# Row norms scaled ahead of the transposes, three tiles deep

## The reference

```python
def rms_norm(x, g):
    xf = x.astype(jnp.float32)
    y = xf * lax.rsqrt(jnp.mean(xf * xf, axis=-1, keepdims=True) + NORM_EPS)
    return (y * g.astype(jnp.float32)).astype(x.dtype)
...
h = rms_norm(x, pre_norm_w[l])
p = h @ w_cat
...
hn = rms_norm_2(h, norm_g)
proj = hn @ w_in
```

## Time and profile before

| What | Value |
|---|---|
| Median of three runs | 3918.17 us |
| Profiled execution, own time | 3913.43 us |
| Its span, first to last instruction | 3911.4 us |
| PE busy | 3361.2 us (86%) |
| DVE busy | 1559.4 us (40%) |
| ACT busy | 1033.8 us (26%) |
| POOL busy | 382.6 us (10%) |
| Mean bandwidth of the transfers | 152 GB/s |

### The profile page before, as it was taken

One profiled execution on the slowest core, in us unless ns is written; L12 is line 12 of the kernel. 1 busy time (PEld: TensorE's weight loads), 2 busy tenths in 40 slices (PEclk: granted clock), 3 DMA queues, 4 the chain that ended last, 5 costly groups with the idle time before them and its releaser, 6 DMA issues. The chain is left out here.

```text
span 3911.4 us, 80384 instructions
## 1 busy us (share of the span) xinstructions
PE 3361.2 (86%) x33244; PEld 2811.4 (72%) x33244; DVE 1559.4 (40%) x2571; ACT 1033.8 (26%) x2007; POOL 382.6 (10%) x407
## 2 busy tenths in 40 slices
PE   7999999888869859999997699999967894988873
PEld 5877777788747749998996488888857873544441
DVE  3145653333336541114665255555433434111113
ACT  2122311122132120012454144455422110211112
POOL 0000000000000000000000122233111000222222
PEclk9999999999989979999998699999978996999997
DMA  3335455211244333233553211111004336999997
GB/s 108 97 115 200 156 199 185 87 52 45 95 167 130 133 94 92 87 97 121 174 171 122 98 33 39 40 50 39 25 21 155 127 101 242 417 419 418 412 415 301
DMA packets 315891, 594.55 MB, mean 152 GB/s; under 512 B 57281, under 2 KB 223018, under 8 KB 286646
## 3 DMA queue, kind: packets, MB, share of 16 engines
q1 hardware_dynamic: 267257, 465.55, 33.6%
q10 hardware_dynamic: 37476, 108.51, 7.9%
q0 software_dynamic: 10928, 17.08, 1.2%
HBM read 471.84 MB, written 139.97 MB: 156 GB/s over the span
## 5 line engine op out<-in xcount | busy, mean ns | idle before, releaser
L3145 PE MATMUL ex_bank_ps<-ex_w_gate_up_sb,ex_xT_sb 128*64 128x256 f32 x2240 | 292.3, 417 | 75.9 <-DMA ex_w_gate_up_sb<-in_w_up_e 68.2
L3145 PEld LDWEIGHTS ex_bank_ps<-ex_w_gate_up_sb,ex_xT_sb 128*64 128x64 f32 x2240 | 171.9, 145 | 208.3 <-issue 127.0
L260 DVE CAST in_w_hi_sb<-in_w_sb 128x1024 fp32r<-128x1024 f32 x119 | 82.0, 689 | 551.3 <-PE in2n_bank_ps L272 268.4
L1428 PE MATMUL mix_bank_ps<-mix_y_hi_sb,mix_wb_hi_sb 128*128 128x512 f32 (+2 forms) x480 | 171.5, 357 | 71.1 <-DVE mix_y_lo_sb L1619 56.0
L272 PE MATMUL in2n_bank_ps<-in_h_hi_sb,in_w_hi_sb 128*128 128x352 f32 (+3 forms) x696 | 224.9, 323 | 3.8 <-DVE in_h_lo_sb L384 3.8
L272 PE MATMUL in2n_bank_ps<-in_h_lo_sb,in_w_hi_sb 128*128 128x352 f32 (+3 forms) x696 | 224.3, 322 | 0.0
L272 PE MATMUL in2n_bank_ps<-in_h_hi_sb,in_w_lo_sb 128*128 128x352 f32 (+3 forms) x696 | 223.8, 322 | 0.0
L272 PE MATMUL qkv_tile_bank_ps<-in_h_hi_sb,in_w_hi_sb 128*128 128x352 f32 (+1 forms) x576 | 192.5, 334 | 8.1 <-DMA qkv_eps_sb<-const_rms_cols 7.5
L3336 DVE TENSOR_TENSOR ex_hidden_sb<-ex_silu_g_sb,ex_bank_ps 128x128 f32<-128x128 f32 x70 | 20.2, 288 | 442.6 <-ACT ex_silu_g_sb L3197 442.6
L272 PE MATMUL qkv_tile_bank_ps<-in_h_lo_sb,in_w_hi_sb 128*128 128x352 f32 (+1 forms) x576 | 185.5, 322 | 0.0
L272 PE MATMUL qkv_tile_bank_ps<-in_h_hi_sb,in_w_lo_sb 128*128 128x352 f32 (+1 forms) x576 | 185.3, 322 | 0.0
(11 more groups left out here) (467 smaller groups left out, 8213.1 us busy)
## 6 DMA issues: line engine op xcount, KB each, us to landing
ex_w_gate_up_sb<-in_w_gate_e SPq DMA_DIRECT2D x70, 1024.0 KB, 20.3
ex_w_gate_up_sb<-in_w_up_e SPq DMA_DIRECT2D x70, 1024.0 KB, 29.7
ex_w_down_sb<-in_w_down_e SPq DMA_DIRECT2D x70, 1024.0 KB, 29.4
in_w_sb<-in_w_in SPq DMA_DIRECT2D x118, 512.0 KB
scr_pT<-in_o_sb ACTq DMA_DIRECT2D x65, 512.0 KB
scr_p2T<-in_o_sb ACTq DMA_DIRECT2D x52, 520.0 KB
qkv_x_sb<-scr_p2T SPq DMA_DIRECT2D x8, 1560.0 KB
mix_gate_sb<-scr_pT SPq DMA_DIRECT2D x24, 512.0 KB, 3.4
```

What stands on the lines that cost most here:

```text
L260: dve.tensor_copy(self.w_hi[:, s, :, 0:width], w).then_inc(self.w_hi_rdy, 1)
L1428: last = pe.matmul(bank[:, 4 * s + c, 0:w], w_[:, s, k, :], y_[:, k0[n] + k, a:a + w], start=(k == 0 and z == 0), stop=(k == kts[n] - 1 an ...
L3145: last = t.matmul(bank[m * BT:(m + 1) * BT, GU_B + b % 2, 0:2 * P], xT[:, s, k, at:at + BT], wgu[:, ws, :, k, m::M], start=(k == 0), stop= ...
```

## The change

In both stages the tile is scaled by `rstd` and by the gain in one instruction of DVE, in token rows and ahead of the transposes. For this the gain is loaded as a row of 1024 numbers, broadcast to all partitions. ACT no longer scales. It casts the transposed tile from PSUM to `h_hi`. DVE subtracts `h_hi` from PSUM to give `h_lo`, so the intermediate `h` is gone.

The loads have four places, the scaled tiles three, the banks four pairs. ACT squares three tiles ahead of its casts, DVE scales three tiles ahead of its subtractions. SP issues the first tile ahead of the constants and leaves the second tile and the gain to ACT's queue. DVE splits the first weights after the first three scalings instead of after the last tile. The loops over tiles are written out.

The core of the diff follows. The call sites pass the gain as the plain vector, and the two arrays that held it in columns are gone.

```diff
     with ExitStack() as ctx:
         st = Stage(nc, ctx, name)
-        h = st.sb("h", [P, 2, KT, rows])
         ident = st.sb("ident", [P, P])
         rms_cols = st.sb("rms_cols", [P, 2])
-        gain_sb = st.sb("gain", [P, KT])
-        x_in = st.sb("x_in", [P, 2, D])
-        junk = st.sb("junk", [P, D])
-        ssq = st.sb("ssq", [P, 2])
-        ms = st.sb("ms", [P, 2])
-        rstd = st.sb("rstd", [P, 2])
-        xn = st.sb("xn", [P, 2, D])
+        gain_sb = st.sb("gain", [P, D])
+        XS, AHEAD = 4, 3
+        x_in = st.sb("x_in", [P, XS, D])
+        junk = st.sb("junk", [P, 2, D])
+        ssq = st.sb("ssq", [P, n_tiles])
+        ms = st.sb("ms", [P, n_tiles])
+        rstd = st.sb("rstd", [P, n_tiles])
+        xn = st.sb("xn", [P, AHEAD, D])
         bank = st.ps("bank", [P, 8, 512])
         consts = st.sem("consts_loaded")
-        x_ld = st.sems("x_loaded")
+        gain_ld = st.sem("gain_loaded")
+        x_ld = st.sems("x_loaded", XS)
         ssq_rdy = st.sem("ssq_ready")
         ms_rdy = st.sem("ms_ready")
         rstd_rdy = st.sem("rstd_ready")
         xn_rdy = st.sem("xn_ready")
         tr_done = st.sem("transposed")
         hT_rdy = st.sem("hT_ready")
-        h_step = st.sem("h_step")
+        hi_rdy = st.sem("h_high_ready")
         block = ctx.enter_context(nc.Block())
         for tiles, _, _ in stretches:
             tiles.psum = lambda s, n: bank[:, 4 * s + n, :]
@@ -331,88 +332,101 @@
                         step(tiles, i, u, width, after)
+        tokens = lambda t: slice(t * rows, (t + 1) * rows)
+
+        turned = lambda t, b: bank[:, 2 * (t % 4) + b, 0:4 * rows].rearrange("p (k r) -> p k r", k=4)
+        first, first_width, _ = stretches[0]
+
+        def load_x(eng, t):
+            if t >= XS:
+                eng.wait_ge(xn_rdy, t - XS + 1)
+            eng.dma_start(x_in[:rows, t % XS, :], src[tokens(t), :]).then_inc(x_ld[t % XS], 16)
+
         @block.sync
         def _(sp):
+            load_x(sp, 0)
+            sp.dma_start(rms_cols[:, :], rms_d).then_inc(consts, 16)
             sp.dma_start(ident[:, :], ident_d).then_inc(consts, 16)
...
+            load_x(sp, 2)
+            first.load(sp, 0, 0, first_width)
+            for t in range(3, n_tiles):
+                load_x(sp, t)
             each_tile(sp, lambda tiles, i, u, width, after: tiles.load(sp, i, u + 1, column=after))
         @block.scalar
         def _(act):
-            act.sem_inc(xn_rdy, 2)
+            load_x(act, 1)
+            act.dma_start(gain_sb[:, :], gain.rearrange("(a d) -> a d", a=1).broadcast_to([P, D])).then_inc(gain_ld, 16)
             stream.begin_store(act)
...
+
+            def square(t):
+                act.wait_ge(x_ld[t % XS], 16 * (t // XS) + 16)
+                act.activation(junk[:rows, t % 2, :], x_in[:rows, t % XS, :], ACT.Square, scale=D ** -0.5,
+                               accum_out=ssq[:rows, t:t + 1]).then_inc(ssq_rdy, 1)
+
+            for t in range(AHEAD):
+                if t >= 2:
+                    act.wait_ge(ssq_rdy, t - 1)
+                square(t)
+            for t in range(n_tiles):
+                act.wait_ge(tr_done, t + 1)
+                for b in range(2):
+                    last = act.activation(h_hi[:, 4 * b:4 * b + 4, tokens(t)], turned(t, b), ACT.Copy)
+                last.then_inc(hi_rdy, 1)
+                if t + AHEAD < n_tiles:
+                    act.wait_ge(ssq_rdy, t + AHEAD - 1)
+                    square(t + AHEAD)
             each_tile(act, lambda tiles, i, u, width, after: tiles.store(act, i, u, width))
             stretches[-1][0].end_store(act)
         @block.vector
         def _(dve):
-            dve.sem_inc(hT_rdy, 2)
             stream.begin_split(dve)
...
+
+            def scale(t):
+                dve.wait_ge(rstd_rdy, t + 1)
+                if t >= AHEAD:
+                    dve.wait_ge(tr_done, t - AHEAD + 1)
+                dve.scalar_tensor_tensor(xn[:rows, t % AHEAD, :], x_in[:rows, t % XS, :], rstd[:rows, t:t + 1], gain_sb[:rows, :],
+                                         ALU.mult, ALU.mult).then_inc(xn_rdy, 1)
+
+            dve.wait_ge(gain_ld, 16)
+            for t in range(AHEAD):
+                scale(t)
+            first.split(dve, 0, 0, first_width)
+            for t in range(n_tiles):
+                dve.wait_ge(hi_rdy, t + 1)
+                for b in range(2):
+                    last = dve.tensor_tensor(h_lo[:, 4 * b:4 * b + 4, tokens(t)], turned(t, b),
+                                             h_hi[:, 4 * b:4 * b + 4, tokens(t)].bitcast(F32), ALU.subtract)
+                last.then_inc(hT_rdy, 1)
+                if t + AHEAD < n_tiles:
+                    scale(t + AHEAD)
+
             each_tile(dve, lambda tiles, i, u, width, after: tiles.split(dve, i, u + 1))
         @block.gpsimd
         def _(pool):
...
+            pool.wait_ge(consts, 32)
+            for t in range(n_tiles):
+                pool.wait_ge(ssq_rdy, t + 1)
+                pool.tensor_tensor(ms[:rows, t:t + 1], ssq[:rows, t:t + 1], rms_cols[:rows, 0:1], ALU.add).then_inc(ms_rdy, 1)
+                pool.wait_ge(ms_rdy, t + 1)
+                pool.tensor_tensor(rstd[:rows, t:t + 1], ms[:rows, t:t + 1], rms_cols[:rows, 1:2], ALU.pow).then_inc(rstd_rdy, 1)
         @block.tensor
         def _(pe):
-            pe.sem_inc(tr_done, 2)
             stream.begin_product(pe)
...
+            pe.wait_ge(consts, 32)
+            for t in range(n_tiles):
+                pe.wait_ge(xn_rdy, t + 1)
+                if t >= 4:
+                    pe.wait_ge(hT_rdy, t - 3)
+                for k in range(KT):
+                    last = pe.transpose(turned(t, k // 4)[:, k % 4, :], xn[:rows, t % AHEAD, k * P:(k + 1) * P], ident[:rows, :rows])
+                last.then_inc(tr_done, 1)
+            pe.wait_ge(hT_rdy, n_tiles)
             each_tile(pe, lambda tiles, i, u, width, after: tiles.product(pe, i, u, width))
...
-        norm_project(nc, "in1n", x, SEQ, P, t["pre_norm_cols"], stream,
+        norm_project(nc, "in1n", x, SEQ, P, t["pre_norm_w"][0], stream,
...
-        norm_project(nc, "in2n", resid, LEN, ROWS, t["norm1_cols"], stream,
+        norm_project(nc, "in2n", resid, LEN, ROWS, t["norm1_g_2"][0], stream,
```

More of the change, by code:

```diff
@@ L350, in _ @@
         def _(act):
-            act.sem_inc(xn_rdy, 2)
+            load_x(act, 1)
+            act.dma_start(gain_sb[:, :], gain.rearrange("(a d) -> a d", a=1).broadcast_to([P, D])).then_inc(gain_ld, 16)
             stream.begin_store(act)
-            act.wait_ge(consts, 48)
-            with act.Fori(0, n_tiles // 2) as i:
-                for s in range(2):
-                    act.wait_ge(x_ld[s], i * 16 + 16)
-                    act.activation(junk[:rows, :], x_in[:rows, s, :], ACT.Square, scale=D ** -0.5,
-                                   accum_out=ssq[:rows, s:s + 1]).then_inc(ssq_rdy, 1)
-                    act.wait_ge(rstd_rdy, 2 * i + s + 1)
-                    act.wait_ge(tr_done, 2 * i + s + 1)
-                    act.activation(xn[:rows, s, :], x_in[:rows, s, :], ACT.Copy,
-                                   scale=rstd[:rows, s:s + 1]).then_inc(xn_rdy, 1)
+            def square(t):
[14 more added lines that the diff above has]
+                    square(t + AHEAD)
             each_tile(act, lambda tiles, i, u, width, after: tiles.store(act, i, u, width))
@@ L3433, in laid_out @@
     return {
-        "pre_norm_cols": columns(a["pre_norm_w"][0]),
         "conv_taps_cols": np.ascontiguousarray(a["conv_w"][0].T),
@@ L3439, in laid_out @@
         "rwkv_columns": np.ascontiguousarray(np.stack(per_channel + list(mu[:4 * C_BR].reshape(4, C_BR)), axis=1)),
-        "norm1_cols": columns(a["norm1_g_2"][0]),
         "conv2_taps_cols": np.ascontiguousarray(a["conv_w_2"][0].T),
```

41 lines of the change are left out of this document (removed).

## The result

The changed kernel takes 3897.31 us (median of five runs, 3888.25 to 3900.21). The kernel before took 3915.26 us in the five runs beside it (3910.63 to 3922.3). The medians differ by 17.95 us. The ratio is 0.995, with a 95% interval from 0.9937 to 0.9963, which is 19.6 us less, between 14.5 and 24.7. The forecast was 3892.6 us with a range from 3880 to 3905. The profiled execution took 3900.21 us with a span of 3898.4 us.

The account below looks back on a forecast made before the run. PE bounds the kernel, so each microsecond its first products start sooner is saved: 11.3 us in in1n and 14.3 in in2n make 25.6, from the median 3918.17 to 3892.6 us. The range was 3880 to 3905.

Parts of the forecast that it names:

- What bounds the stages: In in1n and in2n, latency rounds overlap with three tiles in flight, so DVE's work sets the pace; one round is 6.45 us.
- Pace: In the tile loops, DVE's scaling plus two subtractions take 2.65 us a tile in in1n and 2.45 in in2n.
- The start: At each stage's beginning, the first scaling waits for the gain, landing at 7.5 us in in1n (bounds 5.4 and 8.4).
- POOL beside DVE: In the first three tiles, DVE's scaling holds POOL's power and delays the next rstd: 1.1 us a stage.
- The first weights: In in1n, weights split before the first subtraction land at 9 to 10 us; DVE arrives at 12.4, so nothing waits.
- Sums: First products: in1n at 32.2 us, 11.3 sooner; in2n at 1451.2 us, 14.3 sooner.
- From the product to the kernel: Behind the first products, all waits only for PE, so the 25.6 us gained there shorten the whole kernel equally.
- Early clock: Rival: PE's clock rises during the denser transposes before the first products; 32 us saved, 3886 us; chance 0.20.
- Lock step by step: Rival: in both tile loops POOL always meets a DVE scaling; 14.0 us saved, 3904 us; chance 0.14.
- Time given back: Rival: a later stage waits on something that does not move, so time stays near 3915 us; chance 0.05.
- Slower weight stream: Rival: the experts' weights lie elsewhere in memory and stream slower; at 7% it costs 34 us, 3927 us; chance 0.04.

Follow-up runs that it names:

- e6: Changed kernel, but DVE instead of ACT casts the high part out of PSUM; 3913.51 us.
- e11: Changed kernel with squares, scalings and scaled tiles one ahead in place of three; 3964.56 us.
- e3: Changed kernel with squares, scalings and scaled tiles two ahead in place of three; 3898.95 us.
- e1: Changed kernel, but POOL waits only for its own small table and not for the identity matrix; 3887.37 us.
- e2: Changed kernel with all first loads on SP's queue, gain and second tile included; 3897.86 us.
- e5: Changed kernel with the gain copied once into PSUM by ACT and read there by the row scaling, transposes using three bank pairs; 3882.46 us.
- e4: Changed kernel with twelve unused transposes between the last tile's transposes and the first product; 3890.65 us.
- e9: Changed kernel with the edits of e1 and e5 and the twelve unused transposes of e4, in the gain's banks; median 3887.08 us, 0.9927 against the kernel before.
- e10: The changed kernel, unchanged, run again; median 3895.95 us of five runs, 0.9948 against the kernel before.

## Why the prediction was right

**What bounds the stages.** Right. DVE is full at three tiles ahead (9.60 of 9.60 us), more work on it costs its own length (e6), and fewer tiles ahead let the round show: 6.4 us for one tile (e11), 3.2 for each of two (e3), a tile of 2.39 us at three, where the round would allow 2.13.

**Pace.** 2.65 and 2.45 us were predicted, 2.39 and 2.19 measured. Each instruction has the length that the rows of before gave it: the scaling 1.28 us, the pair of subtractions 1.28 us. What failed is the adding of durations. In the timeline of `in1n` the scaling at 16.83 us takes 1.28 us, and the subtractions start at 18.02, 0.09 us before it ends; the next scaling starts at 19.22, 0.08 us before they end. The pair is 1.28 us and not 2 x 0.685. The term of 8 x 2.65 = 21.2 us was 2.1 us too large, and that of `in2n`, 10 x 2.45, 2.6 us.

**The start.** Mis-sized, and with the wrong event as the last one. I had the gain as the last to land, at 7.5 us. It landed 6.8 us after an issue at 1.18 us, within the bounds. But the first scaling started at 9.12 us: POOL's first sum waited for the identity matrix at 8.20 us, since both constants count on one semaphore. The mend (e1) puts the scaling at 7.96 us, on the gain. In `in2n` it is worse. There the first scaling comes 10.81 us after the stage's first issue, where 6.8 was predicted, and here are the two transfers that matter (KB, us from issue to landing):

```profile
in2n_gain_sb<-in_norm_g ACTq DMA_DIRECT2D x1, 512.0 KB, 8.9
...
in2n_ident_sb<-const_ident SPq DMA_DIRECT2D x1, 64.0 KB, 8.9
```

Both took 8.9 us, above my bound of 7.3 from the earlier trace rows. The prediction placed its 6.4 us between two rows by saying that the broadcast of 4.3 us ran nearly alone. It did not: over these 4.3 us the core's DMA engines were busy 0.91 of the time at 340 GB/s, and over the 7.3 us of the other 0.88 at 299 GB/s. The first square, priced by 3.78 us of a load in the only queue then in use, started 4.8 us after its issue in `in1n` and 7.4 in `in2n`; alone in its queue again (e2) it needs 3.6 and 4.45. The sum moved the load to the front and charged nothing for ACT's queue beside it. The Trainium skill (Trainium Kernel Development and Optimization, "Key Constraints") says that transfers from several engines' queues run on the same 16 DMA engines and that only the issue time is saved; e2 agrees, with 1.5 us on the gain.

**POOL beside DVE.** Right in mechanism and size. The powers beside the second and third scaling took 1.56 and 1.49 us, and DVE lost 2 x 0.44 = 0.88 us, where 1.1 was charged. Later powers that meet a scaling cost nothing: the one of 1.51 us at 17.00 ends at 18.51, and its `rstd` is needed at 19.22. e5 takes the lock away. The Trainium skill (SBUF — State Buffer, "Who interferes with whom") lets an instruction with one input in PSUM leave POOL free, and e5 shows that case, 542 ns.

**The first weights.** Right: the split starts at 13.77 us, right behind the third scaling, with no wait.

**Sums.** The errors cancel in part. `in1n`: start +1.6, pace -2.1, against 32.2 us predicted and 31.63 measured, which is close only by this cancelling. `in2n`: start +4.0, pace -2.6, and 0.4 of a late load near the end (the scalings at 1431.56 and 1434.19 are 2.63 us apart); its saving is 12.1 us, where 14.3 was predicted. The two stages save 24.0 us. That the second product came 26.2 us sooner, close to the predicted 25.6, is luck: 2.2 us of it lie between the stages.

**From the product to the kernel.** The step "Each microsecond by which the first product starts sooner is therefore a microsecond of the kernel" did not hold in full. The medians differ by 17.95 and 20.0 us, and both intervals (to 24.7 and 25.5 us) end below 26.2. The forecast of 3892.6 us lies only 4.7 us from 3897.31 because it was counted from 3918.17, the median of three executions. From the 3915.26 of five it would have been 3889.7, and the miss 7.6. The two solid PE windows behind the products spoke for their own stages and not for the ones that follow. About 1.5 us of the gap are the late taps. For the rest, some 4 us, the profiles leave it open: behind the second product the three profiles of before have 2446.3 us in the mean, the ten of the changed kind (e11 aside) 2451.6, with 4.1 us of standard deviation among them.

**Rivals.** *Early clock:* half of it happened. The last eight transposes of `in1n` took 1.10 us, at the higher level, but PE then stood for 2.80 us and the product started slow again, 13 matmuls. In other profiles, e1 and e4 among them, even these transposes were slow. The prediction's doubt, that the stretch before a product is thin, was the point; e4 and e9 fill it and the product of `in1n` starts fast. *Lock step by step:* fell, DVE has no gap after the third scaling of `in1n`. *Time given back:* true for 1.5 us in q, k and v. *Slower weight stream:* fell, 535.5 against 535.2 us; one of the fourteen profiles, e10, has 3 us more, and the others of either kind lie within 0.5 us.

## What to carry to other kernels

A stage that is a round of latency over several engines is priced by two numbers: the length of the round, and the work of its fullest engine. The number of tiles in flight decides which of the two you pay, so work them out before the depth is chosen (here 6.4 us and 2.4 us, hence three). Where a stage starts with loads, list for its first instruction every semaphore that it waits on: a count shared with a table that the engine never reads held the first scaling by 1.2 us in one stage and 0.9 in the other.

## What the runs showed of the hardware

- DVE's instructions that do not depend on each other overlap by 0.08 to 0.1 us at their ends: a scaling and a pair of subtractions, 1.28 us each by the profile, repeat every 2.39 us. Where the second reads what the first wrote they do not: in e6 the pair of casts takes 1.28 us, and the subtractions that read it start 1.32 us after its start.
- A row scaling of 128x1024 takes 1.28 us with its second input in SBUF or in PSUM alike, but in PSUM it leaves POOL's power its 0.54 us (e5), where the power takes 1.49 to 1.56 us beside the scaling with both in SBUF.
- Where two queues issue a tile at the same moment (512 KB each in `in1n`, 416 in `in2n`), the first comes later than from one queue and the second sooner. The first square started 4.8 and 7.4 us after the issue, against 3.6 and 4.45 with one queue (e2), the second 5.9 and 8.5, against 8.0 and 10.1.
- PE's clock, at the higher level in the last transposes of `in1n` (eight in 1.10 us), was at the lower one after 2.80 us without a matmul (matmuls 0.43 us apart). It was still at the higher one (0.23 us apart) after idle times of 0.80 us (e4) and 1.50 us (e9).
